# One layer step on one core: the order of the launch (modulation chunks, tokens, first weights)

## The reference, cut to what matters

```
sh1, sc1, g1, sh2, sc2, g2 = split(silu(cond) @ w_ada + b_ada, 6)   # w_ada is 1024 x 6144
h = rms_norm(x, norm1_w) * (1 + sc1) + sh1     # cond: c_ctx for context, c for latent tokens
q, k, v, gu, gv = split(h @ w_in, 5)           # w_in is 1024 x 2560
x = x + g1 * (concat([attention(q, k, v), spatial_gating(gu, gv)]) @ w_out)
h2 = rms_norm(x, norm2_w) * (1 + sc2) + sh2
x = x + g2 * moe(h2)                           # 16 experts, top 2 of one group
```

## Time and profile before

| | |
|---|---|
| median of 3 runs | 610.65 us |
| the profiled execution, its own time | 610.96 us |
| its span (first to last instruction) | 609.2 us |
| mean granted TensorE clock | 0.934 of full |
| busy TensorE, VectorE, ScalarE, GpSimd | 520.6, 413.0, 279.9, 189.1 us |
| moved by DMA | 130.98 MB, mean 215 GB/s |

### The profile page before, as it was taken

The page is one execution under the profiler, slowest core; times in us unless marked ns, Lnnn a source line. Parts: engine busy times, 40 slices in busy tenths (PEclk is TensorE's granted clock), DMA queues, the critical chain, the costliest instruction groups (busy, mean ns, idle before and its releaser), DMA issues.

```text
span 609.2 us, 8683 instructions
## 1 busy us (share of the span) xinstructions
PE 520.6 (85%) x2906; PEld 414.5 (68%) x2906; DVE 413.0 (68%) x606; ACT 279.9 (46%) x408; POOL 189.1 (31%) x209
## 2 busy tenths in 40 slices
PE   3799995999999798997899993789999999999800
PEld 3358884898899346655687882368888888888600
DVE  3249666688401678966733667789998989889338
ACT  5046242131311136655600332358888888888400
POOL 2041323211100510000400000526788877874310
PEclk9869997999999999998999986799999999999955
DMA  9993210304271839207456424499596499996666
GB/s 326 387 318 119 82 57 17 139 0 156 71 276 30 301 100 383 73 2 276 167 214 241 174 116 160 157 352 374 212 369 238 183 366 382 381 375 262 231 268 263
DMA packets 41887, 130.98 MB, mean 215 GB/s; under 512 B 6236, under 2 KB 6252, under 8 KB 35584
## 3 DMA queue, kind: packets, MB, share of 16 engines
q1 hardware_dynamic: 32176, 109.62, 48.1%
q0 software_dynamic: 8688, 20.42, 9.7%
q10 hardware_dynamic: 992, 0.55, 0.3%
HBM read 121.35 MB, written 18.38 MB: 229 GB/s over the span
## 4 chain that ended last, share of the span: by engine, by line
PE 70%; DVE 11%; DMA 9%; issue 3%; ACT 2%; SPq 2%; POOL 2%; ACTq 0%; POOLq 0%; DVEq 0%
PE bank L1406 18%; PE bank L1408 18%; PE bank L1407 18%; DMA big<-w_ada 6%; PE bank L1681 3%; PE bank L1525 2%; PE bank L1615 2%; PE bank L1567 2%; SPq L426 1%; DMA big<-w_out 1%; PE bank L1539 1%; PE bank L1549 1%; DVE xt L1097 1%; DVE big L1381 1%; PE bank L1608 1%
## 5 line engine op out<-in xcount | busy, mean ns | idle before, releaser
L1406 PE MATMUL bank<-big_r 128*128 128x512 f32 (+1 forms) x264 | 100.2, 379 | 0.0
L1171 DVE TENSOR_TENSOR big_r<-big,big_r 128x2048 fp32r<-128x2048 f32 x38 | 87.5, 2305 | 5.4 <-ACT big_r L811 5.2
L811 ACT ACTIVATE big_r<-big 128x2048 fp32r (+1 forms) x38 | 72.7, 1917 | 14.8 <-issue 11.4
L1407 PE MATMUL bank<-big_r 128*128 128x512 f32 x200 | 78.9, 395 | 0.0
L1408 PE MATMUL bank<-big_r 128*128 128x512 f32 (+1 forms) x176 | 63.7, 362 | 0.0
L1408 PE MATMUL bank<-big_r,hu_r 128*128 128x512 f32 x160 | 63.0, 394 | 0.0
L1406 PEld LDWEIGHTS bank<-big_r 128*128 128x128 f32 x264 | 54.1, 205 | 7.6 <-issue 1.2
L556 POOL TENSOR_TENSOR small<-small 128x8 f32<-128x8 f32 (+1 forms) x15 | 21.5, 1431 | 82.8 <-DVE small L1005 48.7
L1407 PEld LDWEIGHTS bank<-big_r 128*128 128x128 f32 x200 | 42.1, 211 | 6.3
L633 POOL COPY small<-small 128x1 uint32 x19 | 34.3, 1804 | 23.0 <-ACT rs L871 17.0
L947 DVE TENSOR_TENSOR big_r<-big,big_r 128x1024 fp32r<-128x1024 f32 x28 | 33.5, 1229 | 11.6 <-ACT big_r L698 11.6
(11 more groups left out here) (268 smaller groups left out, 1170.7 us busy)
## 6 DMA issues: line engine op xcount, KB each, us to landing
big<-w SPq DMA_DIRECT2D x32, 1024.0 KB
big<-w_ada SPq DMA_DIRECT2D x12, 2048.0 KB, 14.4
hu<-w SPq DMA_DIRECT2D x16, 1024.0 KB
big<-w_in SPq DMA_DIRECT2D x5, 2048.0 KB, 9.3
big<-slot_out SPq DMA_DIRECT2D x10, 512.0 KB, 7.4
big<-w_out SPq DMA_DIRECT2D x2, 2048.0 KB, 10.6
x_rows<-big SPq DMA_DIRECT2D x5, 512.0 KB, 2.6
h_rows<-vr SPq DMA_DIRECT2D x5, 512.0 KB, 2.6
```

Of the source, the lines that this page charges most:

```text
L811: nc.scalar.activation(w13_hi[p][:, v, :], w13_raw(v, par), ACT.Copy).then_inc(w13_hi_ready, 1)
L1171: V.tensor_tensor(w13_lo[p][:, v, :], w13_raw(v, par), w13_hi[p][:, v, :].bitcast(F32), ALU.subtract).then_inc(w13_lo_ready, 1)
L1406: T.matmul(out, lhs[0], rhs[0], start=start, stop=False)
L1407: T.matmul(out, lhs[0], rhs[1], start=False, stop=False)
```

## The change

SyncE issues the four `w_ada` blocks first, then the tokens, then the `w_in` blocks. TensorE does all four `ada` and `columns` steps first and turns the tokens behind them, with two pairs of banks instead of three. VectorE copies all four modulation results, and makes `colB`, before it starts on the tokens; `colA` is made behind the copies of the last turned tile. In the first row group ScalarE writes `hT_hi` of an even k ahead of the piece of `w_in` for that pair, and VectorE makes value and rest of an even k ahead of the rest of the piece.

```diff
 # SyncE
-            for t in range(TILES):
-                sp.dma_start(x_sb[:, t, :], tile_rows(x_prompt, x_sample, t)).then_inc(x_in[t], 16)
             for key, slot, _ in chunks:
                 kind, j = key
+                if (kind, j) == ("in", 0):
+                    for t in range(TILES):
+                        sp.dma_start(x_sb[:, t, :], tile_rows(x_prompt, x_sample, t)).then_inc(x_in[t], 16)
 # ScalarE
-                nc.scalar.activation(hT[:, 0:4, t * P:(t + 1) * P], banks[2 * (t % 3)][:].rearrange(
+                nc.scalar.activation(hT[:, 0:4, t * P:(t + 1) * P], banks[2 * (t % 2)][:].rearrange(
...
                 for k in range(KD):
+                    if cnd == LAT and k == 0:
+                        act.wait_ge(cols_ready, 2)
+                        act.wait_ge(xT_act, TILES)
+                        act.wait_ge(xT_dve, TILES)
+                    nc.scalar.activation(hT_hi[:, k, ts], ...).then_inc(hT_hi_ready, 1)
                     if cnd == LAT and k % 2 == 0:
                         split_hi(("in", 0), k // 2, win_hi)
-                        if k == 0:
-                            act.wait_ge(cols_ready, 2)
-                            act.wait_ge(xT_dve, TILES)
-                    nc.scalar.activation(hT_hi[:, k, ts], ...).then_inc(hT_hi_ready, 1)
 # VectorE: the loop over ada_copied and colB now stands here, ahead of
             for t in range(TILES):
                 dve.wait_ge(ss_ready, t + 1)
                 V.tensor_scalar(xms[:, t:t + 1], xss[:, t:t + 1], 1.0 / D, EPS, ALU.mult, ALU.add).then_inc(ms_ready, 1)
...
             copy_xT(TILES - 1)
+            dve.wait_ge(col_done, 4)
+            link(V.tensor_tensor(colA, col, b, ALU.add))
+            link(V.tensor_scalar(colA, colA, 1.0, None, ALU.add))
+            V.tensor_tensor(colA, colA, n1w.unsqueeze(2).to_broadcast((P, KD, 2)), ALU.mult).then_inc(cols_ready, 1)
...
                 for k in range(KD):
-                    if i == 0 and k % 2 == 0:
-                        split_lo(("in", 0), k // 2, (win_hi, k // 2 + 1), win_lo)
                     dve.wait_ge(hT_hi_ready, KD * i + k + 1)
...
+                    if i == 0 and k % 2 == 0:
+                        split_lo(("in", 0), k // 2, (win_hi, k // 2 + 1), win_lo)
 # TensorE
-            (turning the tokens, then a wait for all their copies)
             for j in range(4):
                 ada(j)
                 if j:
                     columns(j - 1)
             columns(3)
+            for t in range(TILES):
+                pe.wait_ge(xn_ready, t + 1)
+                if t >= 2:
+                    pe.wait_ge(xT_act, t - 1)
+                    pe.wait_ge(xT_dve, t - 1)
+                xrow = x_sb[:, t, :].rearrange("p (c k) -> p k c", k=KD)
+                for k in range(KD):
+                    ins = T.transpose(banks[2 * (t % 2) + k // 4][:, (k % 4) * P:(k % 4 + 1) * P], xrow[:, k, :],
+                                      ident[:])
+                ins.then_inc(xT_done, 1)
             for _ in range(2):
                 keep_busy(banks[4][:])
```

More of the change, by code:

```diff
@@ L702, in _ @@
                 for k in range(KD):
+                    if cnd == LAT and k == 0:
+                        act.wait_ge(cols_ready, 2)
+                        act.wait_ge(xT_act, TILES)
+                        act.wait_ge(xT_dve, TILES)
+                    nc.scalar.activation(hT_hi[:, k, ts], hT[:, k, ts], ACT.Identity, scale=colA[:, k, cnd:cnd + 1],
+                                         bias=colB[:, k, cnd:cnd + 1]).then_inc(hT_hi_ready, 1)
                     if cnd == LAT and k % 2 == 0:
                         split_hi(("in", 0), k // 2, win_hi)
-                        if k == 0:
-                            act.wait_ge(cols_ready, 2)
-                            act.wait_ge(xT_dve, TILES)
-                    nc.scalar.activation(hT_hi[:, k, ts], hT[:, k, ts], ACT.Identity, scale=colA[:, k, cnd:cnd + 1],
-                                         bias=colB[:, k, cnd:cnd + 1]).then_inc(hT_hi_ready, 1)
             for piece in range(4):
@@ L924, in copy_xT @@
                 dve.wait_ge(xT_done, t + 1)
-                V.tensor_copy(hT[:, 4:8, t * P:(t + 1) * P], banks[2 * (t % 3) + 1][:].rearrange(
+                V.tensor_copy(hT[:, 4:8, t * P:(t + 1) * P], banks[2 * (t % 2) + 1][:].rearrange(
                     "p (k n) -> p k n", n=P)).then_inc(xT_dve, 1)
@@ L931, in _ @@
                             ALU.add).then_inc(fold_ready, 1)
[L932 to L940, removed]
             def split_lo(key, piece, made, ready):
@@ L956, in _ @@
                     V.tensor_copy(ada_s[:, half * 512:(half + 1) * 512], banks[6 + half][:]).then_inc(ada_copied, 1)
-                dve.wait_ge(col_done, 2 * v + 2)
+                if v == 0:
+                    dve.wait_ge(col_done, 2)
                 col = banks[5][:, 0:16].rearrange("p (k c) -> p k c", c=2)
@@ L961, in _ @@
                     V.tensor_tensor(colB, col, b, ALU.add).then_inc(cols_ready, 1)
[L962 to L965, removed]
+            for t in range(TILES):
+                dve.wait_ge(ss_ready, t + 1)
+                V.tensor_scalar(xms[:, t:t + 1], xss[:, t:t + 1], 1.0 / D, EPS, ALU.mult, ALU.add).then_inc(ms_ready, 1)
+                dve.wait_ge(rstd_ready, t + 1)
+                V.tensor_scalar(x_sb[:, t, :], x_sb[:, t, :], xr[:, t:t + 1], None, ALU.mult).then_inc(xn_ready, 1)
+                if t >= 2:
+                    copy_xT(t - 2)
+            copy_xT(TILES - 2)
+            copy_xT(TILES - 1)
+            dve.wait_ge(col_done, 4)
+            link(V.tensor_tensor(colA, col, b, ALU.add))
+            link(V.tensor_scalar(colA, colA, 1.0, None, ALU.add))
+            V.tensor_tensor(colA, colA, n1w.unsqueeze(2).to_broadcast((P, KD, 2)), ALU.mult).then_inc(cols_ready, 1)
             dve.wait_ge(cols_ready, 2)
@@ L1421, in _ @@
             pe.wait_ge(ones_ready, 4)
[L1423 to L1432, removed]
             pe.wait_ge(silu_ready, 1)
@@ L1445, in columns @@
                 ins.then_inc(col_done, 1)
-            pe.wait_ge(xT_act, TILES)
-            pe.wait_ge(xT_dve, TILES)
             for j in range(4):
```

## The result

The changed kernel takes 614.29 us in the median of 20 runs (610.58 to 616.66), the kernel before 610.86 us in 20 runs beside them (608.78 to 614.37). The ratio is 1.005, 95% interval 1.0034 to 1.0067: slower by some 3 us (2.1 to 4.1). The profiled execution took 614.53 us, span 612.8, 3.57 more than before.

The account below looks back on a forecast made before the run. The prediction took the kernel as a chain along TensorE, its start set by VectorE's token loop; +2.9 for the first matmul and -0.2 for the clock gave +2.7, forecast 613.3 us from the median 610.65, range 610.3 to 615.6.

Parts of the forecast that it names:

- The chain: Launch: VectorE's token loop, queued behind the fourth modulation copy, sets the first projection matmul at 45.7 against 42.80, +2.9.
- The step from colA to the matmul: First row group: hT_hi, value and rest, then the rest of the w_in piece take 3.5 us, against 2.6 before.
- The landings: SyncE's queue: last w_ada chunk at 26.2, tiles 27.5 to 33.0, w_in still 38.4; could be off by a microsecond.
- The two pairs of banks: TensorE's turning: each tile waits for the copies two tiles back; priced 0 to 0.3 us, 0.2 taken.
- The row group's order: First row group: w_in's piece now stands behind the tokens of an even k; costs 0.9 us.
- The clock: Start of the projection: likelier at full clock, against a fall during TensorE's pause; -0.2 us taken, bounds -0.85 to +2.
- the launch's shift 1 to 1: Whole kernel: a shift of the first projection matmul moves the end by as much, as TensorE is the chain.
- half clock through all the turning: Rival, TensorE's turning: tile 4 ends at 41.8, first matmul 46.6, +3.8; 614.5 to 615.5 us; chance 0.19.
- full clock early: Rival, TensorE's ada: 1.92 in place of 3.08, first matmul 44.4, +1.6; 611.4 to 612.3 us; chance 0.14.
- the loads decide: Rival, VectorE's loop keeps pace with the landings: first matmul 41.9, -0.9, with full clock -1.7; 609 us; chance 0.08.

Follow-up runs that it names:

- tokens_first_load: Changed kernel with only SyncE's order put back, token loads ahead of the w_ada chunks; 619.43 us, ratio 1.0146.
- means_ahead: Changed kernel with each tile's mean on VectorE placed one tile ahead of the scaling; 610.52 us in one execution.
- load_alone: Kernel before with only SyncE's load order changed (w_ada chunks, then tokens), TensorE still turning tokens first; 628.01 us, ratio 1.0281.
- after_trimmed: Changed kernel with means one tile ahead, three pairs of banks and colA made ahead of the last tile's copy; 613.07 us, ratio 1.0031.
- rows_alone: Kernel before with only the first row group's new order on ScalarE and VectorE; 611.9 us in one execution.
- rows_undone: Changed kernel with the first row group's old order put back, w_in pieces ahead of an even k's tokens; 613.9 us in one execution.
- warm_before: Kernel before with one filler call behind columns(1) and one behind columns(0); 611.09 us, ratio 0.9978, unclear.
- launch_trimmed: Kernel before with columns(1), columns(2) issued before ada(2), ada(3), one filler, and w_in's first pair of k split singly; 613.62 us, ratio 1.004.
- after_filled: Changed kernel with five filler calls instead of two behind the turning; 613.47 us, ratio 1.0035.

## Why the prediction was right

**The chain.** VectorE's token loop behind the fourth copy set the end of the launch, as forecast. The steps, forecast and measured: end of the fourth copy 30.05 and 30.37; last mean 37.3 and 37.73; last tile scaled 38.9 and 39.29; start of tile 4's turning 39.6 and 40.04; last copy 41.6 and 41.89; colA ready 42.2 and 42.41; first matmul 45.7 and 45.99. The step from colA to the matmul, 3.5, measured 3.58. `tokens_first_load` shows by intervention that the loop hangs on the copy and not on the loads, and `means_ahead` that its round trips were on the path, though for less than 1 us beyond TensorE's own row. One slip of the sum is inside these figures: tile 4, started at 39.6 and turned in 1.16, ends at 40.8 and not at 40.9.

**The landings.** The last w_ada chunk was to land at 26.2. It was there when TensorE came to it: ada(3) starts at 26.78 directly behind the columns, with some 0.2 us of waiting; in `means_ahead`, where nothing held TensorE, it starts at 26.64 behind a wait for the chunk. So it landed 0.4 to 0.6 later than I had it. The tiles were to land from 27.5 to 33.0 and did from 28.0 to 34.1. The w_in block was to land at 38.4 as before and landed at 39.5. All loads were late, by 0.4 to 1.1 us, at the edge of the microsecond allowed. The forecast hung on the same bytes arriving at the same rate. The stretches below, before and then after, show that less is moved at first when the queue begins with the 2 MB chunks instead of the five tiles (columns as the earlier trace rows).

```profile
3.00:4.00 1.00, 0.00 (x0) 0.00 (x0) 0.00 (x0) 1.00 (x1) 0.00 (x0) 1.00 1.03 396
```

```profile
3.00:4.00 1.00, 0.00 (x0) 0.00 (x0) 0.00 (x0) 0.59 (x1) 0.00 (x0) 1.00 0.78 254
```

Over the first 8 us the mean is 273 GB/s before and 221 after, which leaves 0.42 MB unmoved, 1.1 us at 386 GB/s. That is the size of the delay, but the slow start isn't shown to be its whole cause: in `load_alone`, just as slow at first (229), w_in was there at 38.3. There the second w_in block was issued only at 43.8, so nothing stood behind the first on SyncE's queue. The delay cost nothing, as ScalarE came to its w_in piece only at 43.16. In a launch bound by w_in it would have.

**The two pairs of banks** were priced at 0.2. Tile 4 waited 0.94 us for a copy; the tile itself was scaled by 39.29, so of 40.04 up to 0.75 is the pairs' doing. The step was mis-sized by half a microsecond, because VectorE's third copy came behind the last scaling; `after_trimmed`, with three pairs, turned the five tiles in 6.17 us without a break, but it moved colA too, so the pairs' share isn't separate.

**The row group's order** was priced at 0.9. By itself it is 0.84 (`rows_alone`), in place 0.37 (`rows_undone`); the other 0.6 by which this distance exceeds 2.60 comes with ScalarE's last copy, which the old order would have met as well. The sum was right, since it ran along the new order; what was wrong is that it put all of the difference down to the edit.

**The clock** was given -0.2 between -0.85 and +2. At the start of the projection it was -0.55 in the profiled execution: the first k took 2.89 in place of 3.44. That this trace started and stayed at full clock is luck as far as the record goes. Three of the five traces with the same kind of pause lost the clock. They took 1.0 to 2.3 us more than the kernel before up to the first squares (21.62 to 22.96 against 20.64), so the upper bound of 2 was somewhat low as well. In the changed kernel the granted clock rose to full during the turning, with nothing but transposes since 33.03, as two stretches of its profile show. The Trainium skill (TensorE: Matmul & The Clock Gate, Part 4: PE-mode transpose) says that full clock doesn't engage for transposes in TensorE's transpose mode. The trace records these only as MATMUL and doesn't show whether that mode was on, so it speaks against the rule for this kernel's transposes and not for every kind.

```profile
35.00:36.00 1.00, 1.00 (x7) 1.00 (x6) 0.75 (x2) 0.85 (x3) 0.12 (x1) 0.50 1.06 391
38.00:39.00 1.00, 1.00 (x10) 0.91 (x9) 0.46 (x1) 0.60 (x1) 0.50 (x1) 1.00 1.06 389
```

**The whole.** Forecast +2.7 in the profiled execution, measured +3.57, with 2.64 of it there after the first k. That this is so near 2.7 is in part two errors that cancel: the first matmul came 0.3 later than forecast, and the clock gave back 0.35 more. The other 0.9 came later, 0.8 of it by 113.8 us, around a stretch in which the granted clock was 0.84 (103 to 123 us) against 0.87 (100 to 120 before). I counted the launch's shift 1 to 1 and had no term for how the clock falls in later stages; that the launch's shift changes it in a given direction isn't shown, and between executions the whole kernel varies by more. Against the medians, +3.43, the shift is within the uncertainty (2.1 to 4.1).

Of the rivals, half clock through all the turning didn't come, nor full clock early; that the loads decide is refuted by `tokens_first_load` for the changed kernel, and `after_trimmed` shows that it would not even be so with VectorE relieved.

## What to carry to other kernels

Moving a load to where it is needed later doesn't remove work from the launch: what was done for free while the other loads arrived (here 10.7 us of VectorE and 7 us of TensorE) comes to stand behind the last landing. Before reordering loads, add up for each engine what its program has left after the last of them, in both orders; the tokens' tail was longer than the modulation's. A step that a faster or slower clock can follow is priced from several traces: one trace with a full clock behind a pause (here two of five) doesn't make it the rule. A serial loop with a round trip to another engine is best placed where something else is being waited for, or with the first half of the next turn ahead of the wait.

## What the runs showed of the hardware

- The queue started slower with the large chunks: 254 GB/s against 396 in the stretch from 3 to 4 us, both near 390 after 10 us. All twelve traces agree over the first 8 us: a mean of 221 to 229 GB/s in the six with the chunks first, 265 to 278 in the six with the tokens first. The first w_in block landed 1.1 us later with the same bytes ahead of it (39.5 against 38.4), but at 38.3 in `load_alone`.
- Small matmuls with two columns (the columns steps) took 3.55 us for a pair of steps in every trace of the kernels that issue the two back to back, at half and at full granted clock alike: from 36.03 in the kernel before, at 0.50, and from 36.15 in `warm_before`, mostly at 1.00.
- The clock at the start of the projection was full behind a pause of 3.1 us in the changed kernel and half for 6 us in `launch_trimmed` behind one of 0.94 us, where TensorE had worked at half clock since 26 us and had one filler call less. The same 12 matmuls of the first k took 2.89 us in the former and 5.25 us in the latter. In `after_trimmed`, behind a pause of 2.8 us, the clock fell from full to half at 43.8 us, and they took 5.28 us.
- Ahead of the first change of clock that a trace records, the granted clock reads 1.00 also where the work ran at the pace of half clock: the first ada of the changed kernel, at 10.62 us, took 3.57 us, against 1.92 us for the second and 3.64 us for the ada at 26.85 us of `after_filled`, wholly at 0.50. So the early rows, among them, are better read by durations than by the granted clock beside them.
